# Weight chunks handed between three engines in two halves of four K tiles, with the K tile as the outer loop of a chunk

## What is computed

```python
def first_block(x, c, ...):                      # 2 layers
    mod = silu(c) @ w_ada[l] + b_ada[l]          # shifts, scales and gates of 6 x 1024
    h = rms_norm(x, norm_mix[l]) * (1.0 + sc1) + sh1
    proj = h @ w_in[l]                           # 1024 x 7440
    ...                                          # conv, delta rule, attention
    merged = sigmoid(gate_a) * (o_dn @ w_dn_out[l]) + sigmoid(gate_b) * (attn @ w_swa_out[l])
    x = x + gt1 * (merged @ w_o[l])
    h = rms_norm(x, norm_ffn[l]) * (1.0 + sc2) + sh2
    up_act, up_lin = split(h @ w_up[l])          # 1024 x 5632
    x = x + gt2 * ((silu(conv(up_act)) * up_lin) @ w_down[l])
def second_block(x, ...):                        # 2 layers
    x = x + 0.5 * swiglu(rmsnorm(x), w_gate1[l], w_up1[l], w_down1[l])
    x = x + hybrid_mixer(rmsnorm(x), w_in_2[l], ..., w_out_2[l])
    x = x + 0.5 * swiglu(rmsnorm(x), w_gate2[l], w_up2[l], w_down2[l])
```

## Time and profile before

| | before |
|---|---|
| median of three runs | 2229.76 us |
| the profiled execution, its own time | 2228.63 us |
| its span in the trace | 2226.8 us |
| PE busy | 2145.2 us (96%) |
| PEld busy | 2043.7 us (92%) |
| DVE busy | 1505.3 us (68%) |
| ACT busy | 1077.0 us (48%) |
| POOL busy | 580.9 us (26%) |
| mean granted clock of PE, share of full | 0.992 |

### The profile page before, as it was taken

How to read it: one execution, slowest core, us unless ns; L and a number is a source line. 1 busy time by engine, 2 the same in 40 slices (tenths; PEclk the granted TensorE clock), 3 DMA queues, 4 the chain that set the end, 5 groups by cost and what they waited for, 6 DMA issues and landing times.

```text
span 2226.8 us, 39796 instructions
## 1 busy us (share of the span) xinstructions
PE 2145.2 (96%) x17221; PEld 2043.7 (92%) x17221; DVE 1505.3 (68%) x1850; ACT 1077.0 (48%) x1432; POOL 580.9 (26%) x280
## 2 busy tenths in 40 slices
PE   7999999999999999999999999989999999999999
PEld 4988899899998888989999999879999999879999
DVE  6967775787678766667666556876556556786555
ACT  3666573433356647443445435554445444555333
POOL 0963324899248260475000000100000000100000
PEclk9999999999999999999999999999999999999999
DMA  9752336677656315566555555335555555434553
GB/s 320 236 170 81 108 121 198 225 252 239 205 181 216 96 41 168 171 213 205 188 184 176 186 184 166 110 96 189 189 188 172 189 184 177 133 95 149 182 185 129
DMA packets 332856, 383.93 MB, mean 172 GB/s; under 512 B 12551, under 2 KB 315402, under 8 KB 332554
## 3 DMA queue, kind: packets, MB, share of 16 engines
q1 hardware_dynamic: 332234, 381.23, 53.6%
q10 hardware_dynamic: 448, 0.16, 0.0%
HBM read 380.32 MB, written 1.05 MB: 171 GB/s over the span
## 4 chain that ended last, share of the span: by engine, by line
PE 75%; DVE 15%; ACT 7%; issue 3%; DMA 0%; SPq 0%; ACTq 0%; DVEq 0%
PE bank L753 16%; PE bank L754 15%; PE bank L755 15%; DVE weights_low L1441 6%; PE bank L993 5%; PE bank L992 5%; PE bank L991 5%; ACT weights_high L2178 4%; DVE arena L1569 2%; PE bank L769 1%; PE bank L892 1%; PE bank L1210 1%; PE bank L1225 1%; PE bank L884 1%; PE bank L1047 1%
## 5 line engine op out<-in xcount | busy, mean ns | idle before, releaser
L1441 DVE TENSOR_TENSOR weights_low<-ring,weights_high 128x2048 fp32r<-128x2048 f32 (+1 forms) x304 | 759.2, 2497 | 431.6 <-ACT weights_high L2178 431.0
L753 PE MATMUL bank<-h_high,weights_high 128*128 128x256 f32 x3296 | 937.9, 285 | 23.7 <-DVE weights_low L1441 14.3
L755 PE MATMUL bank<-h_high,weights_low 128*128 128x256 f32 x3296 | 925.8, 281 | 0.0
L754 PE MATMUL bank<-h_low,weights_high 128*128 128x256 f32 x3296 | 923.0, 280 | 0.0
L2178 ACT ACTIVATE weights_high<-ring 128x2048 fp32r<-128x2048 f32 (+1 forms) x304 | 582.2, 1915 | 693.3 <-PE bank L755 537.1
L753 PEld LDWEIGHTS bank<-h_high,weights_high 128*128 128x128 f32 x3296 | 622.0, 189 | 43.4 <-DVE weights_low L1441 23.8
L754 PEld LDWEIGHTS bank<-h_low,weights_high 128*128 128x128 f32 x3296 | 620.6, 188 | 3.4 <-issue 3.3
L755 PEld LDWEIGHTS bank<-h_high,weights_low 128*128 128x128 f32 x3296 | 620.3, 188 | 0.0
L991 PE MATMUL bank<-hidden_high,weights_high 128*128 128x256 f32 x1056 | 295.3, 280 | 1.4 <-DVE hidden_low L1707 0.9
L993 PE MATMUL bank<-hidden_high,weights_low 128*128 128x256 f32 x1056 | 296.2, 281 | 0.0
L992 PE MATMUL bank<-hidden_low,weights_high 128*128 128x256 f32 x1056 | 295.2, 280 | 0.0
(11 more groups left out here) (439 smaller groups left out, 2817.7 us busy)
## 6 DMA issues: line engine op xcount, KB each, us to landing
ring<-in_w_in SPq DMA_DIRECT2D x80, 1024.0 KB, 5.3
ring<-in_w_up SPq DMA_DIRECT2D x44, 1024.0 KB, 5.3
ring<-in_ffn_w_gate SPq DMA_DIRECT2D x44, 1024.0 KB, 5.4
ring<-in_ffn_w_up SPq DMA_DIRECT2D x44, 1024.0 KB, 5.4
ring<-in_ffn_w_down SPq DMA_DIRECT2D x44, 1024.0 KB, 5.0
side<-in_w_ada SPq DMA_DIRECT2D x42, 1024.0 KB, 7.8
ring<-in_w_down SPq DMA_DIRECT2D x22, 1024.0 KB, 5.0
ring<-in_w_dn_out SPq DMA_DIRECT2D x8, 1024.0 KB, 5.2
```

What stands on the lines that cost most here:

```text
L753: mm(o[:, m, :], a_, high[:, t, :], start=(t == 0), stop=False)
L754: mm(o[:, m, :], a_, low[:, t, :], start=False, stop=False)
L755: last = mm(o[:, m, :], b_, high[:, t, :], start=False, stop=(t == KT - 1))
L1441: v.tensor_tensor(low, wide(q), high.bitcast(F32), ALU.subtract).then_inc(chunk_split, 1)
```

## The change

Each chunk is handed over in two halves of four K tiles (1024 of 2048 columns). ACT rounds a half at a time: the first half once the chunk two before has had its first half multiplied (a new semaphore `half_multiplied`), the second once that chunk is multiplied to its end. DVE lowers a half at a time behind it. PE waits for each half when it comes to it. For this the K tile becomes the outer loop of `linear3`, `linear3_tiles` and `token_major3`, with m or tt inside, so both output groups of a bank are open at once. The waits for `norm_ready` stay one per K tile. The slot is given back to SP after the second half. A chunk whose layout differs (`s1`, 272 columns) waits for the end of the chunk two before in both halves. Counts of `chunk_split` and `chunk_rounded` double.

```diff
@@ PE, linear3 (linear3_tiles and token_major3 alike)
-                pe.wait_ge(chunk_split, n + 1)
...
-                for m in range(2):
-                    for t in range(KT):
-                        if (m, t) == (1, KT // 2) and between is not None:
-                            between()
-                        if norm is not None and m == 0:
-                            pe.wait_ge(norm_ready, KT * norm + t + 1)
...
+                for t in range(KT):
+                    if t % (KT // 2) == 0:
+                        pe.wait_ge(chunk_split, 2 * n + t // (KT // 2) + 1)
+                    if t == 6 and between is not None:
+                        between()
+                    if norm is not None:
+                        pe.wait_ge(norm_ready, KT * norm + t + 1)
...
+                    for m in range(2):
...
+                    if t == KT // 2 - 1:
+                        last.then_inc(half_multiplied, 1)
                 last.then_inc(chunk_multiplied, 1)
@@ PE, down
                 for t in range(2):
+                    pe.wait_ge(chunk_split, 2 * SI[kc, l, i] + t + 1)
                     for m in range(KT):
                         last = down_tile(wh, wl, i, t, m)
-                last.then_inc(chunk_multiplied, 1)
+                    last.then_inc(*((half_multiplied, 1) if t == 0 else (chunk_multiplied, 1)))
@@ DVE, split
-                    dve.wait_ge(chunk_rounded, n + 1)
                     high, low = halves(n)
-                    v.tensor_tensor(low, wide(q), high.bitcast(F32), ALU.subtract).then_inc(chunk_split, 1)
+                    for h, ts in enumerate(HALVES):
+                        dve.wait_ge(chunk_rounded, 2 * n + h + 1)
+                        v.tensor_tensor(low[:, ts, :], wide(q)[:, ts, :], high[:, ts, :].bitcast(F32), ALU.subtract).then_inc(chunk_split, 1)
@@ ACT, split
-                    if n >= 2:
-                        act.wait_ge(chunk_multiplied, M[SPLIT[n - 2]] + 1)
-                    a_(halves(n)[0], wide(q), ACT.Copy).then_inc(chunk_rounded, 1)
+                    for h, ts in enumerate(HALVES):
+                        if n >= 2 and h == 0 and SPLIT[n][0] != "s1":
+                            act.wait_ge(half_multiplied, n - 1)
+                        elif n >= 2:
+                            act.wait_ge(chunk_multiplied, M[SPLIT[n - 2]] + 1)
+                        a_(halves(n)[0][:, ts, :], wide(q)[:, ts, :], ACT.Copy).then_inc(chunk_rounded, 1)
```

More of the change, by code:

```diff
@@ L430, in build @@
         chunk_split = sem("chunk_split")
+        half_multiplied = sem("half_multiplied")
         h_scaled = sem("h_scaled")
@@ L615, in halves @@
             return WH[n % 2][:, :, :], WL[n % 2][:, :, :]
+        HALVES = (slice(0, KT // 2), slice(KT // 2, KT))
         landed = {}
@@ L775, in token_major3 @@
                 wh, wl = halves(n)
-                pe.wait_ge(chunk_split, n + 1)
                 if key in R:
                     pe.wait_ge(*release(PREV[key]))
-                for tt in range(2):
-                    for t in range(KT):
-                        if norm is not None and tt == 0:
-                            pe.wait_ge(norm_ready, KT * norm + t + 1)
-                        a_, b_ = h_high[:, t, tt * P:(tt + 1) * P], h_low[:, t, tt * P:(tt + 1) * P]
-                        mm(dst(tt), a_, wh[:, t, :], start=(t == 0), stop=False)
-                        mm(dst(tt), a_, wl[:, t, :], start=False, stop=False)
-                        last = mm(dst(tt), b_, wh[:, t, :], start=False, stop=(t == KT - 1))
+                opens = lambda t, tt: t == 0 and (tt == 0 or key not in R)
+                for t in range(KT):
+                    if t % (KT // 2) == 0:
+                        pe.wait_ge(chunk_split, 2 * n + t // (KT // 2) + 1)
+                    if norm is not None:
+                        pe.wait_ge(norm_ready, KT * norm + t + 1)
+                    for tt in range(2):
+                        a_, b_ = h_high[:, t, tt * P:(tt + 1) * P], h_low[:, t, tt * P:(tt + 1) * P]
+                        mm(dst(tt), a_, wh[:, t, :], start=opens(t, tt), stop=False, skip_group_check=True)
+                        mm(dst(tt), a_, wl[:, t, :], start=False, stop=False, skip_group_check=True)
+                        last = mm(dst(tt), b_, wh[:, t, :], start=False, stop=(t == KT - 1), skip_group_check=True)
+                    if t == KT // 2 - 1:
+                        last.then_inc(half_multiplied, 1)
                 last.then_inc(chunk_multiplied, 1)
@@ L1009, in last_down @@
                             last = down_tile(wh, wl, FP - 1, t, m)
+                            if (t, m) == (0, KT - 1):
+                                last.then_inc(half_multiplied, 1)
                     if u < 3:
@@ L1410, in _ @@
                 for i in range(4):
-                    linear3_tiles(("out", l, i), merged_high, merged_low, range(KT), pairs if i == 0 else None, (m_split, l + 1))
+                    linear3_tiles(("out", l, i), merged_high, merged_low, pairs if i == 0 else None, (m_split, l + 1))
                 ffn("g2", "u2", "d2", l, ni + 2, 3 + 2 * l)
@@ L2664, in _ @@
             pool.wait_ge(k_landed, 16)
-            pool.wait_ge(chunk_split, SI["qkv", 0, 1] + 1)
+            pool.wait_ge(chunk_split, 2 * SI["qkv", 0, 1] + 2)
             for l in range(LAYERS):
```

39 lines of the change are left out of this document (21 added, 18 removed).

## The result

The changed kernel takes 2233.22 us (median, 2230.11 to 2237.20), the kernel before 2229.28 in the same comparisons (2224.49 to 2230.83). The ratio is 1.0023, 95% interval 1.0017 to 1.0030. I had forecast 2199.5 us and a range of 2184 to 2219, so the forecast is wrong, in size and in sign. The span of the profiled execution is 2228.5 us, 1.7 us more than before; it is one of the shorter executions of the changed kernel, 2.9 us under the median.

What follows compares the result with a forecast made beforehand. PE was taken as the bound, busy 96% of the span, with 29.3 us of waits for lowered weights; gains 25 + 2.2 + 4.2 + 2.8 less 4 made 30.2 us, so 2199.5 us, range 2184 to 2219.

Steps and rivals of the forecast that it cites:

- Extra work: All 304 chunks: halving adds 61 us on ACT and 50 us on DVE, nearly all hidden by idle time.
- Where it costs: `qkv` chunks, delta rule and attention work: extra DVE time that cannot be hidden costs 4 us, bounds 0 and 10.
- Slower: Rival, 4%: doubled fixed cost at 60 chunks, 0.2 us each on DVE, with the ring's gain lost to contention; 2242 us.
- the ring: `swo` chunks: the PE, DVE, ACT cycle of waits falls from 6.12 to 5.47 us, below PE's 5.63.
- The change does little: Rival, 8%: DVE throughput beside POOL bounds the stretches, so earlier hand-over gains nothing; 2228 us.
- The hand-over: PE's waits for lowered weights, 29.3 us: handing over halves removes nearly all; 25 us taken, bounds 15 and 29.
- The second block's norms: Four places (g1 and s2, two layers): PE continues with the next chunk's first half, 1.05 us each, 4.2 us gained.
- The `out` chunks: Two waits for `attended_low`: 24 matmuls ahead instead of 12 gain 1.4 us each, 2.8 us in all.
- The first block's norms: Three places: less work behind the last K tile, partly lost to a lower clock; 2.2 us gained, bounds 0 and 7.5.
- Waits added on PE: One more PE wait per chunk, for the second half, ready before it is needed; cost 0.
- the equal pace of both orders: Blocks of 48 matmuls: switching the output every third matmul costs nothing, blocks still take 5.63 us.

Runs made afterwards that it cites:

- e2: The changed kernel with the lowering whole again on DVE, rounding still in halves; 2213.18 us, ratio 0.9938 to the kernel before.
- e1: The changed kernel with rounding and lowering whole again, only the new matmul order (K tile outside) left; 2225.89 us, ratio 0.9992 to the kernel before.
- e6: The changed kernel with each large GpSimd step of the modulation sums cut in two, lowering still in halves; 2199.53 us, ratio 0.9871 to the kernel before.
- e3: The kernel before without the three large steps of GpSimd's modulation sums; 2205.09 us, ratio 0.9897 to the kernel before.

## Why the prediction was wrong, point by point

*Extra work* and *Where it costs*: **this step failed**, and it carried the sign. I wrote "with the contention that lifts the mean of a lowering to 2.493 ... perhaps 0.17" and 4 us for "Where it costs". The mean treats contention as a slowing of all lowerings by 9%. In fact some lowerings wait until a GpSimd instruction has ended, and cutting a lowering in two gives it two such waits: 62 became 122. The rows to see it were there: L1441 with a median of 2293 and a maximum of 4462 ns. Measured price of DVE's halves in the GpSimd part: 35.4 us net (e2 against the changed kernel), where I allowed 10 at most. At `qkv` I had DVE's work per chunk go from 5.45 to 5.62 us, just below PE's 5.63; measured it is 63.29 x 48 / 479 = 6.3 us, and PE waits.

*Slower*, the rival at 4%: it named the mechanism, "two instructions per chunk meet POOL instead of one", but let it cancel only the ring's gain and priced a meeting at 0.2 us. In the pair above it is nearly 1.6 us (2.79 - 1.22), and DVE's 68% for the whole span, the reason against the rival, is no measure for the stretches with GpSimd. By time (2242) it missed too, since the rest gained more than it let stand.

*The change does little*, the rival at 8% with 2228 us, is nearest to the measured 2233, but by luck: it had neither a loss of 24 us nor a gain of 22. What it said of `qkv`, that DVE's throughput with GpSimd beside it is the bound, is so.

*The hand-over*: right in mechanism; the ring is at 5.63 us. It holds only where GpSimd is silent. In the GpSimd part PE's waits for weights came back longer, 42 us for 27; in the rest they are gone.

*The second block's norms*: the way was right, PE goes on with the first half of the next chunk, but the size was too small. At the four places the changed kernel gains 2.9, 2.7, 2.7 and 2.7 us on the kernel before, read at the same matmul in both, against 1.05 each. e1 and e2 (rest 1143.3 and 1141.2) show that nearly nothing of it comes from the order alone.

*The `out` chunks*: forecast 2.8 us for both layers, measured 3.8 and 5.3. With the norms that is 20 of the 22 us gained in the rest, where the forecast had 7 beside its term for the hand-over. The wait at the turn to the second half fell from 1.6 to 0.77 us; most of the rest must be the ring's gain among those chunks, which I had booked under the hand-over. This split was not tested. PEld of the changed kernel there:

```profile
1502.09 0.19 PEld L735 LDWEIGHTS bank<-attended_high,weights_high 128*128 128x128 f32 x1 [0.77 <-issue]
```

*The first block's norms*: the three places gained 2.0, 1.4 and 1.3 us, 4.7 in sum against 2.2 forecast, each read at the same matmul in both kernels from the start of the chunk to the start of the next. I had the clock fall to its lower level behind the idle time. At the first place (411 us, the feed-forward of the first layer) it did not, but stayed at 1.00, the 2.4 GHz level. PEld, and the window over it (us, then PE, PEld, DVE, ACT, POOL busy, granted clock, DMA share, GB/s):

```profile
411.39 0.19 PEld L760 LDWEIGHTS bank<-h_high,weights_high 128*128 128x128 f32 x1 [2.30 <-issue]
...
417.94 0.19 PEld L760 LDWEIGHTS bank<-h_high,weights_high 128*128 128x128 f32 x1 [0.39 <-issue]
```

```profile
411.40:417.00 5.60, 5.58 (x43) 5.44 (x44) 5.42 (x14) 3.89 (x7) 0.23 (x1) 1.00 0.00 0
```

At the same place of the second layer, in the same execution and with the same order of matmuls, it did fall, behind the same 2.30 us of idle time:

```profile
997.05 0.19 PEld L760 LDWEIGHTS bank<-h_high,weights_high 128*128 128x128 f32 x1 [2.30 <-issue]
```

```profile
997.00:1000.00 3.00, 2.92 (x14) 2.95 (x15) 3.00 (x8) 1.79 (x4) 0.00 (x0) 0.55 0.01 2
```

The two chunks take 417.94 - 411.39 = 6.55 and 1004.22 - 997.05 = 7.17 us up to the next chunk's start, where the kernel before needed 8.51 at both (404.01 to 412.52, and 977.61 to 986.12), with a stretch at the lower level in both. So the fall costs 0.6 us here, and 1.3 us of the gain comes without the clock: PE no longer stands idle between the tiles of the chunk. The Trainium skill ("TensorE: Matmul & The Clock Gate", section "Loop structure matters more than you think") has the loop nest decide whether the clock stays up; by that rule the term would have been 7.5 us. The trace does not bear this out: with one nest the clock was at 1.00 at 411 us and at 0.55 at 997, and e1, with the same nest and whole chunks, shows the reverse (0.64 from 405 to 408 us, 1.00 from 979.6 to 982.6). At the third place, the norm ahead of the second layer's mixer, it fell too. What decides stays open.

The gain at the first place was given back soon: behind a wait of 2.4 us for a contended lowering the clock falls where it had been high, at the 1.2 GHz level.

```profile
426.06 0.19 PEld L760 LDWEIGHTS bank<-h_high,weights_high 128*128 128x128 f32 x1 [2.42 <-issue]
```

```profile
427.50:431.00 3.50, 3.50 (x20) 3.50 (x19) 2.81 (x3) 2.20 (x3) 3.50 (x3) 0.55 0.24 64
```

*Waits added on PE*, at 0, and the equal pace of both orders: right. Between 1100 and 1150 us PE is full in both kernels with one matmul's difference. Before:

```profile
1100.00:1150.00 50.00, 50.00 (x428) 50.00 (x427) 31.96 (x33) 19.97 (x16) 0.00 (x0) 1.00 0.57 186
```

After:

```profile
1100.00:1150.00 50.00, 50.00 (x429) 50.00 (x428) 31.60 (x41) 20.88 (x23) 0.00 (x0) 1.00 0.53 172
```

## What to carry to other kernels

Before cutting an instruction of DVE into pieces, look at what GpSimd does in the same microseconds: if an instruction's maximum is its median plus about a GpSimd instruction, each piece can wait for a turn of its own. Price such a cut from single contended instructions, stage by stage, never from a mean over the span; and where the stages differ, cut only in the stage without GpSimd (here 1.4% faster, where cutting everywhere was 0.2% slower). If it must be cut beside GpSimd, make GpSimd's instructions shorter too.

## What the runs showed of the hardware

- The lowering on DVE and GpSimd's instructions of the sums do not share time but alternate by whole instructions: every lowering that lasts over 0.3 us longer than an undisturbed one ends a fixed time behind the end of a GpSimd instruction, 2.1 to 2.3 us for a whole one (62 of them), 1.1 for a half (122) and 0.55 for a quarter (145).
- The engine whose pieces are cut shorter loses and the other gains. Lowering in 304, 608 and 1216 instructions: 759.2, 879.2 and 974.2 us on DVE, 580.9, 544.9 and 478.5 us on GpSimd. Halves with GpSimd's steps cut in two (e6): 832.7 us and 605.7. Of the 120 us that halves add on DVE some 40 are the fixed part of more instructions (next point).
- With GpSimd's large steps gone, a half takes 1.245 us in the mean over 608, and cutting costs only the fixed part: 741.7 us against the 700.8 us (304 whole ones) of e3.
- Behind the same 2.30 us of idle time and with the same order of matmuls the granted clock stayed at 1.00 at one place (411 us) and fell to 0.55 at another (997 us) of one execution. With half the matmuls behind each tile it fell to 0.51.
